# Modulation rows of a two-block transformer: 64 rows scaled and added by VectorE in one instruction each

## The reference

```python
c_act = silu(c)                                   # [1, 2048]
mod = c_act @ ada_w + ada_b                       # ada_w: [2048, 6*2048]
sh1, sc1, g1, sh2, sc2, g2 = split(mod, 6)
h = rms_norm(x, mix_pre_g) * (1 + sc1) + sh1
q, k, v, a, g = split(h @ w_in)
u = silu(layer_norm(causal_depthwise_conv(a * sigmoid(g), conv_w, conv_b)))
x = x + g1 * rms_norm(concat(attn(q, k, v), u) @ w_out, mix_post_g)
h = rms_norm(x, ffn_pre_g) * (1 + sc2) + sh2
x = x + g2 * rms_norm((silu(h @ w_gate) * (h @ w_up)) @ w_down, ffn_post_g)
```

## Time and profile before

| | |
|---|---|
| three runs, median (lowest to highest) | 2951.14 us (2947.03 to 2952.39) |
| profiled execution, span from first to last instruction | 2948.4 us; the page gives no other time for it |
| PE busy | 2641.7 us, 90% |
| DVE busy | 1927.0 us, 65% |
| ACT busy | 1335.6 us, 45% |
| POOL busy | 421.1 us, 14% |
| moved from memory | 541.68 MB, 184 GB/s over the span |
| L514, the additions on POOL | 64, 263.2 us busy |
| L674, the scalings on ACT | 64, 127.6 us busy |
| L1202, the additions on DVE | 48, 30.1 us busy |

### The profile page before, as it was taken

How to read it: one execution, slowest core, us unless ns; L and a number is a source line. 1 busy time by engine, 2 the same in 40 slices (tenths; PEclk the granted TensorE clock), 3 DMA queues, 4 the chain that set the end, 5 groups by cost and what they waited for, 6 DMA issues and landing times.

```text
span 2948.4 us, 54904 instructions
## 1 busy us (share of the span) xinstructions
PE 2641.7 (90%) x20839; PEld 2577.7 (87%) x20839; DVE 1927.0 (65%) x2464; ACT 1335.6 (45%) x1758; POOL 421.1 (14%) x265
## 2 busy tenths in 40 slices
PE   3477777688999999999899999999999999999997
PEld 2477777687999999999788989999889999999996
DVE  6899989758666666666664455554476666666665
ACT  2354455445444444444454444443454444444443
POOL 0145444424100000000400000000300000000003
PEclk8688888898999999999899999999999999999998
DMA  9766666543666666666444445665445555555552
GB/s 349 289 232 213 231 220 219 184 145 115 215 198 202 198 202 198 202 199 199 123 142 137 135 121 172 182 183 173 152 138 177 184 185 173 185 184 180 183 179 92
DMA packets 458751, 544.89 MB, mean 185 GB/s; under 512 B 15313, under 2 KB 445057, under 8 KB 446112
## 3 DMA queue, kind: packets, MB, share of 16 engines
q1 hardware_dynamic: 448288, 474.07, 51.4%
q0 software_dynamic: 9216, 67.11, 6.5%
q10 hardware_dynamic: 1168, 2.65, 0.3%
HBM read 541.68 MB, written 2.10 MB: 184 GB/s over the span
## 4 chain that ended last, share of the span: by engine, by line
PE 73%; DVE 13%; issue 7%; ACT 3%; POOL 1%; DMA 1%; ACTq 1%; DVEq 1%; SPq 0%; POOLq 0%
PE bank L1578 23%; PE bank L1579 23%; PE bank L1580 23%; DVE w_lo L1010 3%; DVE cv L1163 2%; ACT w_hi L559 1%; DVE y L1106 1%; DVE cvb L1163 1%; DVE acc L1052 1%; DVE acc_b L1052 1%; PE bank L1667 1%; POOL rstd L488 1%; PE bank L1629 1%; DVE rstd L1067 1%; DVE acc L1202 1%
## 5 line engine op out<-in xcount | busy, mean ns | idle before, releaser
L1010 DVE TENSOR_TENSOR w_lo<-raw,w_hi 128x1024 fp32r<-128x1024 f32 x836 | 1124.8, 1356 | 745.2 <-ACT w_hi L559 744.3
L1578 PE MATMUL bank<-h_hi,w_hi 128*128 128x256 f32 (+2 forms) x4496 | 1293.6, 288 | 82.6 <-DVE w_lo L1010 60.7
L559 ACT ACTIVATE w_hi<-raw 128x1024 fp32r<-128x1024 f32 x836 | 877.9, 1058 | 1002.4 <-PE bank L1580 951.4
L1579 PE MATMUL bank<-h_lo,w_hi 128*128 128x256 f32 (+2 forms) x4496 | 1287.7, 286 | 0.0
L1580 PE MATMUL bank<-h_hi,w_lo 128*128 128x256 f32 (+2 forms) x4496 | 1283.3, 285 | 0.0
L1578 PEld LDWEIGHTS bank<-h_hi,w_hi 128*128 128x128 f32 x4496 | 867.4, 193 | 89.5 <-DVE w_lo L1010 48.6
L1579 PEld LDWEIGHTS bank<-h_lo,w_hi 128*128 128x128 f32 x4496 | 867.8, 193 | 0.0
L1580 PEld LDWEIGHTS bank<-h_hi,w_lo 128*128 128x128 f32 x4496 | 867.5, 193 | 0.0
L1578 PE MATMUL bank<-hid_hi,w_hi 128*128 128x256 f32 x1408 | 402.5, 286 | 8.9 <-DVE hid_lo L1343 6.1
L1579 PE MATMUL bank<-hid_lo,w_hi 128*128 128x256 f32 x1408 | 400.5, 284 | 0.0
L1580 PE MATMUL bank<-hid_hi,w_lo 128*128 128x256 f32 x1408 | 400.3, 284 | 0.0
(11 more groups left out here) (199 smaller groups left out, 2436.4 us busy)
## 6 DMA issues: line engine op xcount, KB each, us to landing
raw<-in_w_in SPq DMA_DIRECT2D x210, 512.0 KB, 3.8
raw<-in_w_ffn_up SPq DMA_DIRECT2D x176, 512.0 KB, 4.4
ada_raw<-in_ada_w POOLq DMA_DIRECT2D x64, 1024.0 KB, 6.2
raw<-in_w_gate SPq DMA_DIRECT2D x88, 512.0 KB, 4.6
raw<-in_w_up SPq DMA_DIRECT2D x88, 512.0 KB, 3.5
raw<-in_w_down SPq DMA_DIRECT2D x88, 512.0 KB, 3.5
raw<-in_w_ffn_down SPq DMA_DIRECT2D x88, 512.0 KB, 4.5
ada_pre<-in_ada_w SPq DMA_DIRECT2D x32, 1024.0 KB, 7.2
```

Of the source, the lines that this page charges most:

```text
L559: act.activation(w_hi[:, slot], raw[:, slot], ACT.Copy).then_inc(hi_ready, 1)
L1010: dve.tensor_tensor(w_lo[:, slot], raw[:, slot], fp(w_hi[:, slot]), ALU.subtract).then_inc(lo_ready, 1)
L1578: pe.matmul(dst, wh, x_hi(kt), start=first and k == 0, stop=False)
L1579: pe.matmul(dst, wh, x_lo(kt), start=False, stop=False)
```

## The change

The helper `ada_row` moves from ScalarE's list to VectorE's. There it waits for the row's transfer and does the scaling and the addition over all 2048 columns in one SCALAR_TENSOR_TENSOR. The first row of each part is a TENSOR_SCALAR that writes the accumulator, so the clearing of it goes. ScalarE's 64 scalings, GpSimd's 64 additions and VectorE's 48 partial additions are gone. GpSimd keeps the 64 transfers.

```diff
-DVE_COL = 1664
@@ GpSimd
-                    gp.wait_ge(ada_rest, min(before[-1] + 1, 3 * KT))
...
-            for a in range(4 * KT):
-                part, kt = ADA_ROW[a]
-                cols = slice(0, DVE_COL if part < 5 else D)
...
-                gp.wait_ge(ada_scaled, a + 1)
-                if a:
-                    gp.wait_ge(ada_used, a)
-                gp.tensor_tensor(dst[:, cols], dst[:, cols], ada_raw[:, ADA_SLOT[a], cols], ALU.add).then_inc(ada_used, 1)
-                for b in range(ADA_RING, 4 * KT):
-                    if a == max(x for x in range(b) if ADA_SLOT[x] == ADA_SLOT[b]):
-                        ada_load(b)
+            for a in range(ADA_RING, 3 * KT + 4):
+                ada_load(a)
+            sum_squares(KT + AT, SEQ)
+            residual(y1, SB, 0)
+            gp.wait_ge(h_ready, 2 * KT)
+            gp.memset(y[:, :, SB], 0.0).then_inc(y_zero, 1)
+            for a in range(3 * KT + 4, 4 * KT):
+                ada_load(a)
@@ ScalarE
-                act.activation(ada_raw[:, slot], ada_raw[:, slot], ACT.Copy, scale=cact[:, ds(kt)])\
-                   .then_inc(ada_scaled, 1)
...
-                    if n % 2:
-                        ada_row(i * 4 + n // 2, n // 2)
@@ VectorE
+            def ada_row(dst, slot, kt, first=False):
+
+                dve.wait_ge(ada_loaded[slot], slot_loads[slot].next(1, 16))
+                if first:
+                    op = dve.tensor_scalar(dst[:, :], ada_raw[:, slot], cact[:, kt:kt + 1], None, ALU.mult)
+                else:
+                    dve.wait_ge(ada_used, rows.at())
+                    op = dve.scalar_tensor_tensor(out=dst[:, :], in0=ada_raw[:, slot], scalar=cact[:, ds(kt)],
+                                                  in1=dst[:, :], op0=ALU.mult, op1=ALU.add)
+                op.then_inc(ada_used, 1)
+                rows.next()
...
                 for n in range(8):
                     convert()
-                    if n in (2, 4, 6):
-                        rest_row(acc, n // 2 - 1)
+                    if n % 2:
+                        ada_row(acc, n // 2, body * 4 + n // 2, tile is None and n == 1)
                     if tile is not None:
                         conv(tile, 4 * n, 4 * n + 4)
-                rest_row(acc, 3)
...
-            def clear_rest(dst):
-                dve.memset(dst[:, DVE_COL:], 0.0).then_inc(rest_zero, 1)
-                dve.wait_ge(rest_zero, rest_zeros.next())
...
-                        rest_row(acc if k >= 3 else acc_b, k % 3)
+                        ada_row(acc if k >= 3 else acc_b, k % 3, body * 3 + k % 3, pair is None and k % 3 == 0)
...
-                    rest_row(acc if k >= 4 else acc_b, k % 4)
+                    ada_row(acc if k >= 4 else acc_b, k % 4, 12 + k % 4)
@@ VectorE, first feed-forward
-                chunk(0, gate)
-                chunk(0, up)
+                a = 0
+                for read, t in (gate, 0), (gate, 2), (up, 0), (up, 2):
+                    read(0, t)
+                    for n in range(with_ada * (2 - t // 2)):
+                        ada_row(acc, ADA_SLOT[3 * KT + a], a, a == 0)
+                        a += 1
...
                     down(with_ada)
+                    if with_ada:
+                        ada_row(acc, 0, i + a)
@@ TensorE
-                        pe.wait_ge(ada_rest, 16)
```

More of the change, by code:

```diff
@@ L667, in _ @@
                     convert()
[L668 to L673, removed]
-                act.activation(ada_raw[:, slot], ada_raw[:, slot], ACT.Copy, scale=cact[:, ds(kt)])\
-                   .then_inc(ada_scaled, 1)
-            with loop(act, 4, (halves, 8), (done, 8), (banks, 2), *((c, 1) for c in slot_loads)) as i:
+            with loop(act, 4, (halves, 8), (done, 8), (banks, 2)):
                 for n in range(8):
                     convert()
-                    if n % 2:
-                        ada_row(i * 4 + n // 2, n // 2)
                     if n == 4:
@@ L727, in _, with heads1 @@
                                              [(p_t1[:, :], bank[:, B_P, 0:384])], a1_hi, SEQ)
-            def heads1(body, pair):
+            def heads1(pair):
                 banks.pair = 0
@@ L741, in heads1 @@
                                .then_inc(bank_free[b + o], 1)
[L742 to L750, removed]
+            heads1(None)
+            with loop(act, 3, (halves, 12), (done, 12), (banks, 3), (vs, 2), (masked, 2), (pts, 2), (outs, 2)) as i:
+                heads1(i)
             for n in range(16):
@@ L829, in ffn @@
                 first = (gate, 0), (gate, 2), (up, 0), (up, 2)
-                a = 0
                 for read, t in first:
                     read(0, group(), t)
-                    for n in range(with_ada * (2 - t // 2)):
-                        ada_row(a, ADA_SLOT[3 * KT + a])
-                        a += 1
-                with loop(act, NCHUNK - 1, (halves, 24), (done, 24), (banks, 12), (hids, n_hids),
-                          (slot_loads[0], with_ada)) as i:
+                with loop(act, NCHUNK - 1, (halves, 24), (done, 24), (banks, 12), (hids, n_hids)) as i:
                     chunk(i + 1, gate)
                     skip(8, 8)
-                    if with_ada:
-                        ada_row(i + a, 0)
                     chunk(i + 1, up)
@@ L992, in _ @@
             h_tiles(ST)
-            ffn(gate2, up2, 4, 0, 4)
+            ffn(gate2, up2, 4, 4)
             for n in range(8):
@@ L1168, in conv @@
                     steps.next()
+            rows, slot_loads = Count(), [Count() for _ in range(ADA_RING)]
+            def ada_row(dst, slot, kt, first=False):
[8 more added lines that the diff above has]
+                rows.next()
             def gated(body, tile):
@@ L1189, in gated @@
                                       sigg[:, o:o + 1], ALU.mult).then_inc(bank_free[a + o], 1)
-            rests, rest_zeros = Count(), Count()
-            def clear_rest(dst):
-                dve.memset(dst[:, DVE_COL:], 0.0).then_inc(rest_zero, 1)
-                dve.wait_ge(rest_zero, rest_zeros.next())
-            def rest_row(dst, slot):
-                dve.wait_ge(ada_scaled, rests.at(1, 1))
-                if rests.c:
-                    dve.wait_ge(ada_rest, rests.at())
-                dve.tensor_tensor(dst[:, DVE_COL:], dst[:, DVE_COL:], ada_raw[:, slot, DVE_COL:], ALU.add)\
-                   .then_inc(ada_rest, 1)
-                rests.next()
-            clear_rest(acc)
             gated(0, None)
-            with loop(dve, 3, (halves, 8), (done, 8), (banks, 2), (steps, CONV_K + 1), (rests, 4)) as i:
+            with loop(dve, 3, (halves, 8), (done, 8), (banks, 2), (steps, CONV_K + 1), (rows, 4),
+                      *((c, 1) for c in slot_loads)) as i:
                 gated(i + 1, i)
-            clear_rest(acc_b)
             for o in range(2):
@@ L1252, in _, with heads1 @@
                                              128, a1_hi, a1_lo, SEQ)
-            def heads1(pair, tile):
+            def heads1(body, pair, tile):
                 banks.pair = 0
```

34 lines of the change are left out of this document (7 added, 27 removed).

## The result

In the first comparison the changed kernel took **2843.84 us** (median of 4 runs, 2841.91 to 2851.80) against 2951.76 us for the kernel before (4 runs): a ratio of 0.9638, 95% interval 0.962 to 0.9655. It ran in two more comparisons, with medians of 2848.31 and 2846.53 us; over all 14 runs the median is 2846.7 us and the spread 2841 to 2854, while the kernel before kept medians of 2950.7 to 2952.5. So the gain is 105 us, where 89 were forecast. The profiled run took 2842.01 us, of which 2840.2 are the span.

What follows compares the result with a forecast made beforehand. VectorE was taken to bound stages 1 to 4, stalled about 3.75 us by each GpSimd addition, and TensorE the feed-forward. Gains 6.1 + 22.8 + 10.2 + 28.5 + 10.9 + 3.6 + 7.0 = 89.1 us gave 2862 us; range 2846 to 2889.

Steps and rivals of the forecast that it cites:

- a loop body of stage 1: Convolution steps and gate product with four rows: VectorE's list alone, 40.2 us, becomes 32.6; three bodies gain 22.8 us.
- Rivals 1, 3 and 4: 1: transfers, half clock bind, 2891 us, 0.13; 3: rows await transfers, 3040; 4: stalls not additions', 3036; 3+4 0.03.
- Rival 2: More than forecast: fewer clock falls, cheaper first rows, quicker layer norm; gain up to 105 us, 2846 us; chance 0.06.
- the first body of stage 2: Body without attention, six rows: 52.7 us becomes 42.5, from a VectorE list of 40.9; gain 10.2 us.
- stage 5: Feed-forward's first chunk: TensorE's 6.5 us of waits for splits go, plus a little clock; gain 7.0 us.
- Stage 4: Eight subtractions feeding the sum of squares shrink from 6.00 to about 2.8 us, plus 0.4 elsewhere; gain 3.6 us.
- Attention bodies and stage 3: Three attention bodies of stage 2, 56.8 to 47.3 us each, gain 28.5; stage 3, 48.1 to 37.2, gain 10.9.
- Stage 1: First body, near its transfer bound, gains 6.1 us instead of 7.6; three loop bodies gain 22.8 us.
- no VectorE instruction above 2.5 us between 130 and 520 us: Sign in VectorE's timeline that the stalls beside GpSimd's additions are gone.
- The layer norm's sums, expected near 473 us: Sign: their start moves from 551.3 us to near 473, by the 78.5 us of stages 1 to 3.

Runs made afterwards that it cites:

- first two experiments: The changed kernel with idle GpSimd work before each of 60 later transfers: an addition of 1664 columns, 2962.28 us; then two MEMSETs instead, 2853.41 us.
- the fourth: The kernel before, with the border between GpSimd's and VectorE's share of a row at column 832 in place of 1664: 2906.58 us.
- the third: The changed kernel with ScalarE scaling every row in place again and VectorE adding all 2048 columns: 2843.72 us.

## Why the prediction was right in its mechanism and wrong in its sum

The mechanism was right, and its parts were measured one by one: the stall is GpSimd's addition (first two experiments), shares on both engines add up (the fourth), ScalarE's part is worth nothing (the third), and a loop body of stage 1 is VectorE's list and nothing else: 31.9 us in its third and fourth body, against 32.6 forecast. Rivals 1, 3 and 4 did not come about. No row waited for its transfer: the landing stayed at 4.9 to 11.9 us, with a ring's turn of over 20 us. Rival 2, more than forecast, is what happened, and it had been given 0.06.

What failed is the size of terms in the sum of 89.1 us. Two of them failed in every profile by some 4 us: the first body of stage 2 (10.2, measured 14.2 to 14.8), where the two first rows were priced at 2.35 us and last 1.28, and an allowance for the clock was added that was not needed; and stage 5 (7.0, measured 10.9 to 11.2), where the half clock behind TensorE's waits was put at 0.5 us and cost 4.3. By stages:

- **Stage 2, first body** (10.2 forecast, 14.2 to 14.8 measured). "VectorE's list after ... = 40.9", "I take 42.5". Two first rows were priced at 2.35 us and last 1.28: 2.1 us, and the run that put them back was 1.6 to 2.1 us longer here. The four others were priced by length, not by their distance of 2.26: 0.4. The 1.6 added for TensorE's clock was not needed: the clock was 0.96 between 246 and 285 us.
- **Stage 5** (7.0, measured 10.9 to 11.2). "The 6.5 and a little of the clock": the little was 4.3 us, as large as two thirds of the wait itself.
- **Stage 4** (3.6, measured 4.7 to 7.3). The eight subtractions became 2.77 us, as forecast. The 16 matmuls of the sum ahead of them took 3.72 us in two profiles and 6.33 in the third, by the clock; before it was 5.17. That is the whole difference of 2.6 us between the profiles, and the forecast could not foresee which it would be: against the 5.17 of before, 1.5 us of the first profile's surplus are luck.
- **Attention bodies and stage 3** (39.4, measured 41.9 to 42.4). A body took 46.7 to 46.9 us in the mean, where the list was 46.4 and 47.3 was taken: of the 0.9 us "for what doesn't fit" about half was needed. The rows were priced by length here too: 0.5 us a body and 0.4 in stage 3. What the rest of stage 3's 1.1 to 1.4 us comes from is not shown.
- **Stage 1** (28.9, measured 27.9, 28.0 and 32.8). The 1.5 us kept back for transfers in the first body was right in kind; its size differs from execution to execution. The first two bodies took 1.6 to 6.5 us more than in the run with less to load, and this is part of the 13 us by which executions of the changed kernel differ. The other loop bodies are 0.7 us quicker than forecast, 0.36 of it from the 0.09 us by which a row's distance is below its length.

In every profile some 11 us of surplus come from the first body of stage 2 (4.0 to 4.6), the attention bodies with stage 3 (2.5 to 3.0) and stage 5 (3.9 to 4.2). Stage 4 adds 1.1 to 3.7, and stage 1 between -1.0 and 3.9. Between the gain forecast and that of all 14 runs lie 16 us. The common failure: where two sides of a price were known (first row, clock, transfer) the side that gains less was taken each time. Each choice alone was defensible; their sum was not the likeliest value. The sum without any allowance, rival 2's 105 us, was the better estimate.

Of the signs, "no VectorE instruction above 2.5 us between 130 and 520 us" held for single instructions; groups of several in one row of the timeline are longer. The layer norm's sums, expected near 473 us, started at 461.5, 467.9 and 466.1 us.

## What to carry to other kernels

When an engine is busy for a whole stretch, look in its timeline for one instruction that is much longer than its like, and then for what another engine runs between the same two times; if the ends agree, that work is not parallel, and moving it to the engine it stops is a gain as long as its price there is below the stall. After such a gain ask what stands in the way of the next one: rows that are moved into idle time of VectorE gave the time expected, but the 32 small matmuls that they feed have to be placed as well. Inside a wait of TensorE they cost little as long as nobody waits for them; in the middle of its work they cost their own length and slow the matmuls behind them; after an idle stretch they run at half clock. And when several uncertain prices enter one sum, take for each the value nearest to what the rows show, and keep the cautious ends for the range alone.

## What the runs showed of the hardware

- GpSimd's fp32 addition of 128 x 1664 stops VectorE's two-input instructions (3.10 us against 0.40 to the next start); a MEMSET of the same size, 1.49 us, doesn't (478 ns a step, as without it).
- That MEMSET does stop one-input TENSOR_SCALARs of 128 x 256 on VectorE that begin while it runs: up to 1.33 us instead of 0.41, and up to 1.65 instead of 0.35, each ending 0.15 us behind the MEMSET.
- The same addition with both inputs the same takes 3.12 us, with two different ones 3.78 us.
- VectorE's TENSOR_SCALAR on 128 x 2048 fp32 lasts 1.28 us; SCALAR_TENSOR_TENSOR, with two tensors, 2.35 us, and TENSOR_TENSOR 2.28 us.
- 32 matmuls of one column took 4.10 us directly behind a busy stretch and 6.96 us after TensorE had waited. Behind the feed-forward's total, in the first profile after, 14 matmuls started 0.21 us apart instead of 0.12, for 3.1 us. A wait of 6.5 us in five pieces cost another 4.3 us in that way.
- With the transfers 0.91 to 0.95 of the time busy (326 to 343 GB/s), the first body of stage 1 of the same kernel took 32.6, 33.7 and 37.4 us in three executions.
